# Two stacked transformer blocks in fp32: SBUF start addresses of the weight products' operands

## What is computed

```python
def conv_gated_ffn(xn, w_gate, w_up, dw_w, dw_b, w_down):
    g = causal_depthwise_conv(xn @ w_gate, dw_w, dw_b)
    return (jax.nn.gelu(g, approximate=True) * (xn @ w_up)) @ w_down
...
def _even_mixer(h, w_in, f_bias, lam_vecs, subln_g, w_out, layer_idx):
    proj = h @ w_in
...
    return o @ w_out

def _retention(h, w_in, w_out):
    proj = h @ w_in
...
    return y @ w_out

def _sq_relu_mlp(h, w1, w2):
    return jnp.square(jax.nn.relu(h @ w1)) @ w2
```

## The kernel before

| operand | first byte | modulo 256 | step from tile to tile |
|---|---|---|---|
| weights, slot 0 of `whi`, `wlo` | 24,704, 41,344 | 128 | 512 |
| weights, slot 1 | 33,024, 49,664 | 0 | 512 |
| weights `pw_*`, `fw_*`, `gw_*` (a copied chunk each) | | 64, 96, 64 | 512 |
| `x1h`/`x1l`, `f1h`/`f1l`, `g1h`/`g1l`, `qxh`, `ph`: 256 columns | | 64 | 1,024 |
| `xh`/`xl` in even_out and ret_v: 272 columns | 58,112 | 0 | 1,280 |
| the same in ret_g, from column 16: 256 columns | 58,176 | 64 | 1,280 |
| `xrh`/`xrl` in even_dqk, even_v and even_fqk: 272 columns | 204,800 | 0 | 1,280 |
| the same in ffn_up0 and ret_qk's second half: 274 columns | 204,800 | 0 | 1,280 |
| the same in ret_qk's first half and ffn_up1, from column 16: 258 columns | 204,864 | 64 | 1,280 |
| `fh`/`fl` in ffn_down0: 272 columns | 135,168 | 0, 64, 128, 192 in turn | 1,088 |

## Time and profile before

### The profile page before, as it was taken

The page is one execution under the profiler, slowest core; times in us unless marked ns, Lnnn a source line. Parts: engine busy times, 40 slices in busy tenths (PEclk is TensorE's granted clock), DMA queues, the critical chain, the costliest instruction groups (busy, mean ns, idle before and its releaser), DMA issues.

```text
span 1116.8 us, 24238 instructions
## 1 busy us (share of the span) xinstructions
PE 1091.4 (98%) x8961; PEld 1056.4 (95%) x8961; DVE 780.7 (70%) x1403; ACT 621.1 (56%) x1192; POOL 358.2 (32%) x396
## 2 busy tenths in 40 slices
PE   9998999999989999999999999999999999999996
PEld 8976999999989999899999999999989999999996
DVE  5776588887478777767887554795556567987554
ACT  5657566556455657765656334563336646665433
POOL 2102323334302412245666111300034335675120
PEclk9999999999999999999999999999999999999998
DMA  8463447775556623225555545654414565556550
GB/s 240 127 190 114 115 118 211 195 191 164 192 173 196 219 76 114 77 93 172 180 159 187 182 159 185 212 186 154 150 39 152 187 202 175 179 181 204 189 187 38
DMA packets 202938, 180.63 MB, mean 162 GB/s; under 512 B 6864, under 2 KB 200819, under 8 KB 202739
## 3 DMA queue, kind: packets, MB, share of 16 engines
q1 hardware_dynamic: 202179, 175.74, 50.7%
q0 software_dynamic: 688, 3.94, 0.9%
HBM read 176.28 MB, written 1.05 MB: 159 GB/s over the span
## 4 chain that ended last, share of the span: by engine, by line
PE 88%; DVE 5%; ACT 3%; issue 2%; POOL 1%; DMA 1%; SPq 0%; ACTq 0%; DVEq 0%; POOLq 0%
PE ps L1979 26%; PE ps L1980 26%; PE ps L1981 26%; DVE wlo L1342 2%; PE ps L2406 1%; PE ps L2150 1%; PE ps L2536 1%; ACT whi L797 1%; POOL acc L602 1%; PE ps L2514 1%; PE ps L2389 1%; DMA raw<-w_ple_gate 1%; PE ps L2185 1%; PE ps L2364 1%; PE ps L2484 0%
## 5 line engine op out<-in xcount | busy, mean ns | idle before, releaser
L1342 DVE TENSOR_TENSOR wlo<-raw,whi 128x1024 fp32r<-128x1024 f32 x316 | 396.5, 1291 | 152.2 <-ACT whi L797 150.4
L797 ACT ACTIVATE whi<-raw 128x1024 fp32r<-128x1024 f32 x315 | 317.5, 1051 | 157.8 <-PE ps L1981 145.7
L1979 PE MATMUL ps<-xh,whi 128*128 128x256 f32 (+1 forms) x880 | 250.0, 284 | 0.7 <-DVE wlo L1342 0.4
L1980 PE MATMUL ps<-xl,whi 128*128 128x256 f32 (+1 forms) x880 | 247.4, 281 | 0.0
L1981 PE MATMUL ps<-xh,wlo 128*128 128x256 f32 (+1 forms) x880 | 247.3, 281 | 0.0
L1979 PE MATMUL ps<-xrh,whi 128*128 128x274 f32 (+2 forms) x832 | 241.2, 290 | 0.0
L1980 PE MATMUL ps<-xrl,whi 128*128 128x274 f32 (+2 forms) x832 | 238.4, 287 | 0.0
L1981 PE MATMUL ps<-xrh,wlo 128*128 128x274 f32 (+2 forms) x832 | 238.4, 287 | 0.0
L1981 PE MATMUL ps<-fh,wlo 128*128 128x256 f32 (+1 forms) x688 | 193.3, 281 | 0.0
L1980 PE MATMUL ps<-fl,whi 128*128 128x256 f32 (+1 forms) x688 | 193.1, 281 | 0.0
L1979 PE MATMUL ps<-fh,whi 128*128 128x256 f32 (+1 forms) x688 | 193.1, 281 | 0.0
(11 more groups left out here) (371 smaller groups left out, 1618.6 us busy)
## 6 DMA issues: line engine op xcount, KB each, us to landing
raw<-ffn_w SPq DMA_DIRECT2D x128, 512.0 KB, 4.4
raw<-ret_w_in SPq DMA_DIRECT2D x48, 512.0 KB, 4.4
raw<-even_w_in SPq DMA_DIRECT2D x24, 512.0 KB, 4.7
raw<-w_ffn_gate SPq DMA_DIRECT2D x22, 512.0 KB, 4.0
raw<-w_ffn_up SPq DMA_DIRECT2D x22, 512.0 KB, 5.2
...
```

Of the source, the lines that this page charges most:

```text
L797: A(whi[:, slot, s * 1024:s * 1024 + 1024], raw[:, slot, s * 1024:s * 1024 + 1024], ACT.Copy).then_inc(w_hi_ready, 1)
L1342: V.tensor_tensor(wlo[:, slot, s * 1024:s * 1024 + 1024], raw[:, slot, s * 1024:s * 1024 + 1024], f32(whi[:, slot, s * 1024:s * 1024 + 102 ...
L1979: T.matmul(dst, w[0], x[0], start=first, stop=False)
L1980: T.matmul(dst, w[0], x[1], start=False, stop=False)
```

## The change

It moves operands in SBUF. The padding of `whi`/`wlo` between slots goes (slots are 8,192 bytes apart), `xh`/`xl` move to the end of the fixed part, just ahead of the arenas, at a multiple of 512 bytes, and their views begin 16 columns (64 bytes) in. The hidden rows of the first feed-forward net of the second block get tensors of their own, `f0h`/`f0l`, with tiles 1,280 bytes apart, laid over `xh`, `xl` and the arena. `xrh`/`xrl` is read in two views: `xeh`/`xel`, 16 columns in, for the even layer, and `xrh`/`xrl`, 32 columns in, for ffn_up0, ret_qk and ffn_up1. The copied weight chunks move to 128 modulo 256. No instruction is added or taken away. Starts after, modulo 256, with `xh_mem` at 114,176 and the arenas at 134,656:

| operand | before | after |
|---|---|---|
| weights in slot 0, slot 1 | 128, 0 | 128, 128 |
| `pw_*`, `fw_*`, `gw_*` | 64, 96, 64 | 128 |
| 256 columns of `x1`, `f1`, `g1`, `qx`, `p` | 64 | 64 |
| 272 columns in even_out, ret_v | 0 | 64 |
| 256 columns in ret_g | 64 | 128 |
| 272 columns in even_dqk, even_v, even_fqk | 0 | 64 |
| 274 columns in ffn_up0, ret_qk | 0 | 128 |
| 258 columns in ret_qk, ffn_up1 | 64 | 192 |
| 272 columns in ffn_down0 | 0, 64, 128, 192 in turn | 64 (step 1,280) |

```diff
--- before.py
+++ after.py
@@ -53,7 +53,7 @@
 CH = 2048
 UNITS1 = [(t, hd) for t in (1, 0) for hd in range(HEADS)]
 T1_LAG, V1_LAG, N1_LAG = 2, 3, 4
-XS, WS = 320, CH + 32
+XS = 320
 
 
 STAGES = [("qkv_in", 3, 3), ("conv_in", 4, 4), ("q", 2, 4), ("kv", 1, 3), ("ple_w", 1, 0), ("mix_out", 4, 4), ("ple", 0, 4),
@@ -168,18 +168,13 @@
 
 
         raw = sb("raw", [P, 2, CH])
-        whi = sb("whi", [P, 2, WS], F32R)
-        wlo = sb("wlo", [P, 2, WS], F32R)
+        whi = sb("whi", [P, 2, CH], F32R)
+        wlo = sb("wlo", [P, 2, CH], F32R)
         sb("x_lines", [P, 32])
-        xh_mem = sb("xh", [P, KD, XS], F32R)
-        xl_mem = sb("xl", [P, KD, XS], F32R)
-        xh, xl = xh_mem[:, :, 0:N2], xl_mem[:, :, 0:N2]
-
         def short_rows(t, depth, skip=0):
             flat = t[:, :, :].rearrange("p k n -> p (k n)")
             return flat[:, skip:skip + depth * N1].rearrange("p (k n) -> p k n", k=depth)
 
-        x1h, x1l = short_rows(xh_mem, KD, META), short_rows(xl_mem, KD, META)
         h = sb("h", [P, KD, N2])
         y_at = 32 * ((nc.sbuf_base + 31) // 32)
         y = sb("y", [P, KD, N2])
@@ -217,7 +212,13 @@
         wf = sb("wf", [P, KD, 8])
         f_bias = sb("f_bias", [8, 1])
         small = sb("small", [P, 64, 4])
-        arena0 = 512 * ((nc.sbuf_base + 511) // 512)
+        sb("x_pad", [P, -nc.sbuf_base % 512 // 4])
+        f0_at = nc.sbuf_base + 4 * META
+        xh_mem = sb("xh", [P, KD, XS], F32R)
+        xl_mem = sb("xl", [P, KD, XS], F32R)
+        xh, xl = xh_mem[:, :, META:META + N2], xl_mem[:, :, META:META + N2]
+        x1h, x1l = short_rows(xh_mem, KD, META), short_rows(xl_mem, KD, META)
+        arena0 = nc.sbuf_base
 
 
         class Arena:
@@ -230,9 +231,9 @@
                 self.at += 32 * ((size + 31) // 32)
                 return t
 
-        def line_at(byte):
-
-            return byte + (64 - byte) % 256
+        def line_at(byte, start=64):
+
+            return byte + (start - byte) % 256
 
         m1 = Arena()
         xt = m1("xt", [P, 2, D])
@@ -248,10 +249,11 @@
         m1.at = line_at(m1.at)
         ph = m1("ph", [P, 2, N1], F32R)
         pl = m1("pl", [P, 2, N1], F32R)
-        pw_at = m1.at
+        pw_at = m1.at + 64
         qxh = m1("qxh", [P, 5, N1], F32R)
         qxl = m1("qxl", [P, 5, N1], F32R)
         qkv = m1("qkv", [P, 6, N1])
+        m1.at += 64
         sq6 = m1("sq6", [P, 5, N1])
         conv_in = m1("conv_in", [P, CT, SEQ + TG])
         cv = m1("cv", [P, CT, N1])
@@ -260,7 +262,7 @@
         ang = m1("ang", [P, 4, N1])
         turn = m1("turn", [P, 5])
         mask1 = m1("mask1", [P, N1])
-        kt_at = m1.at
+        m1.at = kt_at = line_at(m1.at, 128)
         kt_ = m1("kt", [P, HEADS, N1])
         v1 = m1("v1", [P, 2, HEADS * VDIM])
         lr = nc.alloc_sbuf_tensor_at("lr", [P, 2, N1], F32, offset=m1.at)
@@ -271,7 +273,7 @@
 
         diag_first = nc.alloc_sbuf_tensor_at("diag_first", [P, TG * TS, 32], F32, offset=rows_at)
         assert 4 * TG * TS * 32 <= rows_end - rows_at
-        diag_at = m1.at
+        m1.at = diag_at = line_at(m1.at, 128)
         diag_rest = m1("diag_rest", [P, CT - 1, TG * TS, 32])
         diag = [diag_first[:, :, :]] + [diag_rest[:, m, :, :] for m in range(CT - 1)]
         pw_hi = nc.alloc_sbuf_tensor_at("pw_hi", [P, CH], F32R, offset=pw_at)
@@ -280,16 +282,20 @@
         pw_lo = nc.alloc_sbuf_tensor_at("pw_lo", [P, CH], F32R, offset=pw_at + 4 * CH)
         o_tok = fa[:, :, :].rearrange("p k n -> p (k n)")[:, 0:2 * HEADS * VDIM].rearrange("p (t n) -> p t n", t=2)
         f1 = Arena()
-        fh = f1("fh", [P, FT2, N2], F32R)
-        fl = f1("fl", [P, FT2, N2], F32R)
-        f1h, f1l = short_rows(fh, FT2, META), short_rows(fl, FT2, META)
+        fh_mem = f1("fh", [P, FT2, N2], F32R)
+        fl_mem = f1("fl", [P, FT2, N2], F32R)
+        f1h, f1l = short_rows(fh_mem, FT2, META), short_rows(fl_mem, FT2, META)
+        f0h, f0l = (nc.alloc_sbuf_tensor_at(name, [P, FT2, XS], F32R, offset=f0_at + 4 * n * FT2 * XS)[:, :, 0:N2]
+                    for n, name in enumerate(("f0h", "f0l")))
         xr_at = f1.at
-        gw_hi, gw_lo = (nc.alloc_sbuf_tensor_at(name, [P, CH], F32R, offset=arena0 + at0 + 4 * (META + FT * N1))
+        gw_hi, gw_lo = (nc.alloc_sbuf_tensor_at(name, [P, CH], F32R, offset=arena0 + at0 + 4 * (2 * META + FT * N1))
                         for name, at0 in (("gw_hi", 0), ("gw_lo", 4 * FT2 * N2)))
-        assert META + FT * N1 + CH <= FT2 * N2
-
-        xrh = f1("xrh", [P, KD, XS], F32R)[:, :, 0:N2 + 2]
-        xrl = f1("xrl", [P, KD, XS], F32R)[:, :, 0:N2 + 2]
+        assert 2 * META + FT * N1 + CH <= FT2 * N2
+
+        assert f0_at + 8 * FT2 * XS - 4 * META <= xr_at
+        xr_mem = [f1(name, [P, KD, XS], F32R) for name in ("xrh", "xrl")]
+        xeh, xel = (x[:, :, META:META + N2] for x in xr_mem)
+        xrh, xrl = (x[:, :, 2 * META:2 * META + N2 + 2] for x in xr_mem)
         gt = nc.alloc_sbuf_tensor_at("gt", [P, 2, 2 + N1], F32, offset=xr_at)
         e1 = Arena()
 
@@ -742,7 +748,7 @@
                     low(m, m % 4)
 
             sums(S_LN, y, ALL)
-            hidden(FT, ALL, fh, fl)
+            hidden(FT, ALL, f0h, f0l)
             sums(S_LN + 1, y, ALL)
 
             pool.wait_ge(stat_ready, S_LN + 2)
@@ -1110,7 +1116,7 @@
                 for m in range(2):
                     k = 2 * j + m
                     act.wait_ge(h_ready, KD + k + 1)
-                    A(xrh[:, k, 0:N2], h[:, k, :], ACT.Copy).then_inc(xh_ready, 1)
+                    A(xeh[:, k, :], h[:, k, :], ACT.Copy).then_inc(xh_ready, 1)
             split_at(C0["ple_gate"] + 5, (1,))
 
             def qk_high(c, turn, chunk):
@@ -1252,7 +1258,7 @@
                     high(t, t % 4)
 
             residual(S_LN, "even_out", 1, 0, ALL)
-            ffn_up("ffn_up0", FT, 0, ALL, fh)
+            ffn_up("ffn_up0", FT, 0, ALL, f0h)
             residual(S_LN + 1, "ffn_down0", 4, 1, ALL)
 
             for c in range(8):
@@ -1700,7 +1706,7 @@
                 if j > 0:
                     split_at(C0["ple_gate"] + j + 2, (0, 1) if j < 3 else (0,))
                 for k in (2 * j, 2 * j + 1):
-                    x_low(X_B, k, h[:, k, :], dst=(xrh, xrl))
+                    x_low(X_B, k, h[:, k, :], dst=(xeh, xel))
             split_at(C0["ple_gate"] + 5, (1,))
 
             def qk_low(c, turn):
@@ -1971,7 +1977,7 @@
         @block.tensor
         def _(pe):
             T = nc.tensor
-            rows_x, rows_q, rows_r, rows_f = (xh, xl), (qxh, qxl), (xrh, xrl), (fh, fl)
+            rows_x, rows_q, rows_e, rows_r, rows_f = (xh, xl), (qxh, qxl), (xeh, xel), (xrh, xrl), (f0h, f0l)
             rows_x1, rows_f1, rows_g1 = (x1h, x1l), (f1h, f1l), (g1h, g1l)
 
             def three(dst, w, x, first, last):
@@ -2331,7 +2337,7 @@
                 pe.wait_ge(sig_ready, 2 * j - 2)
                 product(c + j, (c + j) % 2, pair("ple_gate", j, N1), rows_x1, TOK1, 256).then_inc(mm_done, 1)
 
-            outputs("even_dqk", 2, ALL, rows_r, x_from(X_B), qk_ready, lambda j: 2 * j + 2)
+            outputs("even_dqk", 2, ALL, rows_e, x_from(X_B), qk_ready, lambda j: 2 * j + 2)
 
             def qkv_products(c, slot, b, x):
 
@@ -2432,7 +2438,7 @@
                 chunk = C0["even_v0"] + c
                 pe.wait_ge(*freed[c])
                 steps = 2 * KD
-                for n, ins in enumerate(qkv_products(chunk, chunk % 2, 2 * (c % 2), rows_r)):
+                for n, ins in enumerate(qkv_products(chunk, chunk % 2, 2 * (c % 2), rows_e)):
                     if n + 1 == steps:
                         ins.then_inc(mm_done, 1)
                     for k, i in enumerate(WITH[c]):
```

## The result

The changed kernel takes 1,123.05 us (median of 6 runs, 1,122.38 to 1,124.02), the kernel before 1,118.64 us beside it (6 runs, 1,117.89 to 1,119.54). The ratio is 1.0040 with a 95% interval of 1.0027 to 1.0053: slower by 4.4 us where 7.4 us less was forecast. The profiled execution took 1,122.87 us with a span of 1,121.0, 4.2 us over the 1,116.8 of before, so it can be used to find where the 4.4 us lie.

The account below looks back on a forecast made before the run. The prediction took TensorE, busy 98% of the span, as the bound. Its terms, 4.0 + 0.9 + 1.5 + 1.1 + 1.1 + 0 - 1.4 + 0.2 = 7.4 us saved, took 1,118.64 to 1,111.2 us; range 1,105.4 to 1,119.5.

Parts of the forecast that it names:

- Step 9: Block 1, ret_out and ffn_down1 (256 columns): slot 1's weights go from 0 to 128 modulo 256; change 0.
- The case that I gave 0.04: Long stages fall to the second pace (117.7 against 113.3 ns for 256 columns): 3.4 us less saved, 1,114.6 us; chance 0.04.
- step 8: Copied weights pw, fw, gw (48 matmuls each), moved to 128: from 120 to between 113.3 and 117.7 ns, 0.2 us saved.
- Step 6: ffn_up0 and ret_qk's second half, 960 matmuls of 274 columns: stay near 126.8 ns, 0; bounds 5.8 us saved, 6.4 lost.
- Step 1: ffn_down0, 768 matmuls of 272 columns: 125.5 to 120.0 ns, 4.0 us saved after allowing one chunk in the second pace.
- A less W: Moving operand's start less weight tile's start, modulo 256 bytes; claimed to decide how their reads collide, hence the matmul pace.
- Steps 2, 3, 4: 272 columns to 122.2 ns in even_out, ret_v, and even_dqk with even_v and even_fqk: 0.9, 1.5 and 1.1 us saved.
- Step 5: ret_qk's first half and ffn_up1, 960 matmuls of 258 columns: mean 119.9 to 118.8 ns, 1.1 us saved.
- Step 7: ret_g, 384 matmuls of 256 columns, operand and weight starts now equal: about 116.4 to 120.0 ns, 1.4 us lost.
- The rest costs nothing on the path: Whole kernel: no instruction, wait or DMA added, queue order kept, and DVE does not starve the faster PE in ffn_down0.
- No settling: Rival: 272 columns stay near 124 to 125 ns whatever the operand's start; 2.8 us saved, 1,115.8 us; chance 0.19.
- Slower: equality costs in full: Rival: each 274-column matmul with equal starts pays 16 more cycles, 6.4 us lost; 1,122.2 us with no settling; chance 0.10.

Follow-up runs that it names:

- slots in turn again: Changed kernel with the padding back between the weight slots (starts 128 and 0 modulo 256): 1,118.71 us, ratio 0.9988.
- block 1 alone: Changed kernel with weight slot 1 at 0 modulo 256 in the first block only, 128 from there: 1,119.41 us, ratio 1.0004.
- the last version: Changed kernel with weight slots alternating 128/0 (192/64 in ret_g), fixed at 128 from even_dqk to ret_v, and 274 columns at 0: 1,114.95 us, ratio 0.9966.
- both slots at 128: Kernel before with only the padding moved behind the slots, so both weight slots start at 128 modulo 256: 1,127.96 us, ratio 1.0070.
- 274 columns moved: Changed kernel with the 274- and 258-column views starting 16 columns in instead of 32 (at 64 and 128 modulo 256): 1,123.1 us, ratio 1.0042.
- the bare stream: Separate kernel of matmuls only, other engines idle, 96 per combination of column count, weight start and operand start: 272 columns took 123.3 to 126.6 ns.

## Why the prediction was wrong

- **Step 9 failed.** "ret_out runs at 113.3 in both slots: 0" took from the earlier trace rows that W 0 and W 128 are equally good, and missed that their taking turns had an effect: it put the second pace at nothing in stages that had long run at 113.3. Four profiled executions with W in turn in block 1 (before, slots in turn again, block 1 alone, the last version) left the second pace in gate_up after the chunk at 155 to 158 us; three with W fixed (after, both slots at 128, 274 columns moved) kept it to the end of the stage. It cost 3.9 us in gate_up and 2.0 us in down, 5.9 us in all. mix_out (+0.8) and ple_gate (-1.7) are not this step's: the granted clock made +1.2 and -1.1 us of them. What is left, -0.4 and -0.7 us, is the second pace on its other side (the last chunks of both stages were in it before and are at 113.3 ns after) and step 8. ret_out changed by nothing. The case that I gave 0.04, a pace falling to its second value, had the right effect with too small a chance and without its cause.
- **Step 6 failed.** "126.8, which holds for W equal to A too" read the equal slot of the earlier trace rows while the slots took turns. Equality with W fixed is another case: 130.0 ns in these stages. They lost 2.8 + 0.5 = 3.2 us (before rounding), of which 0.6 us is the longer wait for GpSimd. My bound (16 cycles, 6.4 us) held it; the value taken was wrong. The sign was there to be seen: in before, ffn_up0's first chunk, with slot 1 (A and W both 0), ran at 130.0 ns from its third tile on, and the second at 126.7 from its second tile on.
- **Step 1: mechanism right, size off.** A less W is what decides. But I carried "count + 16" over from 256 columns; 272 at -64 settle at 296 cycles, 123.3 ns, in the bare stream too. It measured -1.7 for -4.0.
- **Steps 2, 3, 4** have the same error, less of it, since I had taken 122.2: -0.6, -0.9 and -0.9 for -0.9, -1.5 and -1.1. In step 4 PE gained some 2.2 ns (125.8 to 123.6 in the first three chunks), and of 2.2 × 576 = 1.3 us 0.9 arrived, more than the half that I had counted for the chain through DVE. Of step 2's 0.6 us only 0.1 us arrived at the layer norm, the rest turned into the wait for GpSimd.
- **Step 5: right.** 119.0 ns in ret_qk and ffn_up1 for the 118.8 expected; -0.8 for -1.1.
- **Step 7: right.** ret_g at 120.0 ns with A equal to W, +1.6 for +1.4.
- **Step 8: right in sign.** The chunks with `pw`, with the first of `fw` and with the second of `gw` took 7.58, 6.63 and 5.91 us before and 7.50, 6.52 and 5.67 after, 0.4 us in all; both slots at 128 alone, which left these copies where they were, has the numbers of before, and slots in turn again, which moved them, has 7.48, 6.52 and 5.67.
- **"The rest costs nothing on the path"** held for DVE and the queues in ffn_down0, and failed in ffn_up0, where GpSimd's sum, ready no sooner than before, was waited for 0.6 us longer.

The difference between forecast and trace, 4.2 + 7.4 = 11.6 us, is 5.9 (step 9), 3.2 (6), 2.3 (1), 1.6 (2, 3, 4, 5, 7: 0.3, 0.6, 0.2, 0.3, 0.2), less 0.7 in mix_out and ple_gate beyond step 8's 0.2, and less 0.7 gained at the start and the end. "No settling" had come near in what it gave for 272 columns (124) and was wrong on why: they don't stay there whatever A is, but go from 123.3 to 126.6 by A less W. "Slower: equality costs in full" had the right place with twice the price; that its 1,122.2 us lies near the measured 1,123.05 is luck, since the 5.9 us of gate_up and down are not in it.
